# A mixer-and-experts kernel on one core: the first block's rows made by TensorE, and a token's two expert rows fetched in two turns

## What is computed

```
def _moe(h, router_w, router_b, w1, w3, w2):
    s = jax.nn.sigmoid(t @ router_w)                 # 16 experts in 4 groups
    # the best group, in it the two best experts, weights normed over the two
    gates = ...
    for e in range(N_EXPERTS):
        hid = jax.nn.silu(t @ w1[e]) * (t @ w3[e])   # 1024 -> 256
        y = y + gates[:, e:e + 1] * (hid @ w2[e])    # 256 -> 1024
```

## Time and profile before

| | us |
|---|---|
| median of 3 runs | 1379.61 |
| lowest and highest | 1375.94, 1379.90 |
| the profiled execution, its own time | 1375.57 |
| its span | 1373.8 |
| TensorE busy | 1231.2 (90%) |
| VectorE busy | 839.2 (61%) |
| ScalarE busy | 477.3 (35%) |
| GpSimd busy | 325.0 (24%) |
| mean granted TensorE clock | 0.946 of full speed |

### The profile page before, as it was taken

One profiled execution on the slowest core, in us unless ns is written; L12 is line 12 of the kernel. 1 busy time (PEld: TensorE's weight loads), 2 busy tenths in 40 slices (PEclk: granted clock), 3 DMA queues, 4 the chain that ended last, 5 costly groups with the idle time before them and its releaser, 6 DMA issues.

```text
span 1373.8 us, 24782 instructions
## 1 busy us (share of the span) xinstructions
PE 1231.2 (90%) x9304; PEld 828.1 (60%) x9304; DVE 839.2 (61%) x1616; ACT 477.3 (35%) x974; POOL 325.0 (24%) x388
## 2 busy tenths in 40 slices
PE   2989999999699999699999699999999997899980
PEld 2478867747355454484854388888888555455540
DVE  5578575484367564879325667777774425466654
ACT  4000126203165562201028544444443102466541
POOL 1000019100133333100001343444443000333433
PEclk9899899899699999899999799999999998999995
DMA  9677666482998994411110000000001405999955
GB/s 365 213 245 285 211 236 218 135 294 93 322 373 310 377 324 139 160 62 62 62 61 0 31 3 2 22 2 2 2 3 63 154 0 197 316 379 382 378 156 196
DMA packets 125163, 234.77 MB, mean 171 GB/s; under 512 B 9376, under 2 KB 77168, under 8 KB 125072
## 3 DMA queue, kind: packets, MB, share of 16 engines
q1 hardware_dynamic: 114144, 199.89, 41.9%
q0 software_dynamic: 10752, 33.56, 7.0%
q10 hardware_dynamic: 176, 0.05, 0.0%
HBM read 210.42 MB, written 23.07 MB: 170 GB/s over the span
## 4 chain that ended last, share of the span: by engine, by line
PE 74%; DVE 11%; DMA 8%; issue 3%; ACT 2%; POOL 1%; SPq 1%; DVEq 0%; POOLq 0%; ACTq 0%
PE PS L2142 14%; PE PS L2287 12%; PE PS L2108 8%; PE PS L2305 6%; PE PS L2063 5%; PE PS L2486 2%; PE PS L2468 2%; DMA xn_rows<-arena 2%; PE PS L2036 2%; PE PS L2437 2%; PE PS L2275 2%; PE PS L2374 2%; DMA arena<-in_moe_w 2%; DMA arena<-in_ada_w 2%; DVE arena L1367 2%
## 5 line engine op out<-in xcount | busy, mean ns | idle before, releaser
L2287 PE MATMUL PS<-WR,arena 128*64 128x256 f32 x1536 | 180.5, 389 | 5.2 <-ACT arena L1166 4.5
L2287 PEld LDWEIGHTS PS<-WR,arena 128*64 128x64 f32 x1536 | 108.8, 139 | 61.4 <-ACT arena L1166 6.4
L2142 PE MATMUL PS<-WR,arena 128*128 128x256 f32 x480 | 112.0, 395 | 4.2 <-DVE arena L1788 4.2
L2108 PE MATMUL PS<-WR,arena 128*128 128x512 f32 x256 | 112.6, 596 | 0.0
L2142 PEld LDWEIGHTS PS<-WR,arena 128*128 128x128 f32 x480 | 94.7, 199 | 20.1 <-DVE arena L1788 3.2
L1367 DVE SCALAR_TENSOR_TENSOR arena<-arena,cact 128x1024 f32<-128x1024 f32 x77 | 99.2, 1288 | 12.5 <-DMA arena<-in_ada_w 6.7
L1617 DVE COPY WR<-arena 128x2560 f32 x48 | 71.9, 1498 | 38.7 <-issue 29.3
L2305 PE MATMUL PS<-W,arena 128*64 128x512 f32 x384 | 92.9, 604 | 0.9 <-DVE arena L1643 0.9
L917 POOL DMA_DIRECT2D expert_rows<-arena x96 | 52.0, 541 | 156.9 <-DVE arena L1651 152.6
L2063 PE MATMUL PS<-arena,WR 128*128 128x512 f32 x192 | 86.1, 605 | 1.1 <-DVE arena L1454 1.1
L1150 ACT COPY WR<-arena 128x1536 f32 x48 | 71.0, 1480 | 42.4 <-issue 27.7
(11 more groups left out here) (370 smaller groups left out, 2262.1 us busy)
## 6 DMA issues: line engine op xcount, KB each, us to landing
arena<-in_moe_w SPq DMA_DIRECT2D x96, 1024.0 KB, 12.8
arena<-in_ada_w SPq DMA_DIRECT2D x82, 512.0 KB, 4.6
expert_rows<-arena POOLq DMA_DIRECT2D x96, 128.0 KB, 5.4
WR<-in_rwkv_w_rkv SPq DMA_DIRECT2D x6, 2048.0 KB, 7.8
WR<-in_mix_w_in SPq DMA_DIRECT2D x5, 2048.0 KB, 9.9
WR<-in_mix_w_out SPq DMA_DIRECT2D x2, 2048.0 KB, 7.9
expert_rows<-arena SPq DMA_DIRECT2D x1, 4096.0 KB, 14.3
xn_rows<-arena SPq DMA_DIRECT2D x2, 2048.0 KB, 13.8
```

Of the source, the lines that this page charges most:

```text
L2108: last = mm(out, HT[:, c, b * P:(b + 1) * P], WR[:, (first_tile + half) % 2, c, :], start=(c == 0), stop=(c == KC - 1))
L2142: last = mm(out[:, n * 256:n * 256 + 256], left, right, start=(c == 0), stop=(c == 3))
L2287: last = mm(PS[rows2[h], 2 + n, 0:2 * P].rearrange("p (m f) -> p m f", m=2), XgT[:, n, c, :], w[:, :, c, cols(h)], start=(c == 0), stop=(c ...
```

## The change

Four things are changed in the experts of both layers.

1. **The first item's rows.** As soon as `rank` is known VectorE builds `HOT0`, which marks for each token its place in item 0. TensorE then makes the rows of item 0, already turned, as 32 matmuls of 128x64 (`first_rows`, 16 for the chunks of ScalarE ahead of the list matmuls, 16 for those of VectorE behind them). The gather and the transposes of item 0 go, and so does `keep_warm(..., 5)`; `keep_warm(..., 3)` becomes `keep_warm(..., 1)`. Item 0 always belongs to expert 0, so its weights are staged without waiting for `items`.
2. **The store of `XN`** stands on SyncE's queue ahead of `landed(0)` and `load(3)`. `load(2)` now waits also for the last matmul that reads `XN` (`tx_up`). The three small loads of layer 0 move behind the experts.
3. **The order of a token's rows.** `in_order` (VectorE, 13 small instructions) puts the lower slot of a token first, with the weights to match. The lower slot is never in expert 15, so GpSimd fetches these rows (`pair_in(0)`) once the rows of experts 0 to 14 are written, and the others (`pair_in(1)`) after the last. The adds go block by block over the lower rows and then over the others.
4. **The last item's rows** are written out by SyncE and not by GpSimd.

Some semaphores of the set-up are merged, with no other change there.

```diff
+        HOT0 = tmp[:, 0, 0:NB * ROWS].rearrange("p (b r) -> p b r", b=NB)
...
             tt(A[:, 0:64], rank, m1, ALU.mult)
+            tt(sm[:, 1, 0:NB], sm[:, 0, 0:NB], b3(rank)[:, :, 0], ALU.add)
             link(tt(B[:, 0:64], rank, m2, ALU.mult))
+            tt(HOT0, io128[:, 0:ROWS].unsqueeze(1).to_broadcast([P, NB, ROWS]),
+               sm[:, 1, 0:NB].unsqueeze(2).to_broadcast([P, NB, ROWS]), ALU.is_equal).then_inc(M("idx"), 1)
...
                 load(0)
                 sp.wait_ge(*full("y", 8 * layer + 8))
                 load(1)
+                sp.wait_ge(sem("xn"), NB * (2 * layer + 2))
+                sp.dma_start(xn_dram.rearrange("(b p) f -> p b f", p=P), XN).then_inc(sem("rows_out"), 16)
                 landed(0)
                 if layer == 0:
                     sp.wait_ge(*full("mod", 5))
                 load(3)
                 landed(1)
-                sp.wait_ge(sem("xn"), NB * (2 * layer + 2))
-                sp.dma_start(xn_dram.rearrange("(b p) f -> p b f", p=P), XN).then_inc(sem("rows_out"), 16)
                 sp.wait_ge(sem("rows_out"), 16 * layer + 16)
+                sp.wait_ge(M("tx_up"), 1)
                 load(2)
                 sp.wait_ge(sem("items"), layer + 1)
...
                 landed(NEXP - 1)
+                pairs_of = sp.value_load(CN[0:1, 0:1], min_val=NEXP // 2, max_val=MAX_ITEMS // 2)
+                sp.wait_ge(sem("yt_last"), layer + 1)
+                for h in range(2):
+                    sp.dma_start(rows_of[bass.ds(pairs_of * 2 - 1, 1), h].rearrange("k r f -> (k r) f"),
+                                 Yt[rows2[h], 1, :]).then_inc(sem("last_out"), 16)
             moe(0)
+            sp.dma_start(W1L, io["rwkv_w1"][0].rearrange("(c p) f -> p c f", p=P)).then_inc(sem("lora_in"), 16)
+            sp.dma_start(A1L, io["rwkv_a1"][0].rearrange("(c p) f -> p c f", p=P)).then_inc(sem("lora_in"), 16)
+            sp.dma_start(G1L, io["rwkv_g1"][0].rearrange("(c p) f -> p c f", p=P)).then_inc(sem("lora_in"), 16)
...
-                for j in range(4):
+                for j in range(3):
                     row_out(j % 2, pairs_of * 2 + j - 4)
...
+                gp.wait_ge(sem("ranked"), layer + 1)
+                lower_out = [gp.value_load(CN[0:1, 1 + n:2 + n], min_val=NEXP // 2 - 1, max_val=MAX_ITEMS // 2)
+                             for n in range(2)]
+                def pair_in(j):
+                    for b in range(NB):
+                        gp.indirect_dma_start(CB[j][:, b, :], None, y_dram,
+                                              bass.IndirectOffsetOnAxis(ap=SLI[:, j, b:b + 1], axis=0)
+                                              ).then_inc(sem(f"pair_in{b}" if j else "lower_in"), 16)
+                for n in range(2):
+                    gp.wait_ge(M(f"row_out{n}"), lower_out[n] * 32)
+                gp.reg_add(rows_sent[0], rows_sent[0], 32)
+                gp.wait_ge(sem("rest_out"), 16)
+                pair_in(0)
+                gp.wait_ge(sem("last_out"), 32 * layer + 32)
+                for n in range(2):
+                    gp.wait_ge(M(f"row_out{n}"), rows_sent[n])
+                pair_in(1)
...
-                keep_warm(bank("lbias", layer), 3)
+                keep_warm(bank("lbias", layer), 1)
+                def first_rows(out, chunks):
+                    for k, c in enumerate(chunks):
+                        for b in range(NB):
+                            last = mm(out[:, k * ROWS:(k + 1) * ROWS], XN[:, b, c * P:(c + 1) * P], HOT0[:, b, :],
+                                      start=(b == 0), stop=(b == NB - 1))
+                    return last
+                pe.wait_ge(M("idx"), 1)
+                pe.wait_ge(sem("xn"), NB * (2 * layer + 2))
+                first_rows(PS[:, 6, :], TURN_ACT)
                 pe.wait_ge(sem("hot"), layer + 1)
                 for k in range(8):
                     last = mm(out[:, 0:MAX_ITEMS], HOTR[:, k, :], HOTI[:, k, :], start=(k == 0), stop=(k == 7))
                 last.then_inc(filled["list"], 1)
+                first_rows(PS[:, 7, :], TURN_DVE).then_inc(M("tx_up"), 1)
...
-                keep_warm(PS[:, 5, :], 5)
-                turn(0, 16)
-                pair(lambda d: d, [32, 16], first=True)
+                pair(lambda d: d, [16, 16], first=True)
...
-                for b in range(NB):
-                    v.wait_ge(sem(f"pair_in{b}"), 32 * (layer + 1))
-                    for j in range(2):
-                        if b or j:
-                            v.wait_ge(sem("x_done"), 8 * L + 2 * b + j)
-                        stt(X[:, b, :], CB[:, 2 * b + j, :], W12[:, j, b:b + 1], X[:, b, :], ALU.mult, ALU.add
-                            ).then_inc(sem("x_done"), 1)
+                v.wait_ge(sem("ranked"), layer + 1)
+                for k in range(2 * NB):
+                    j, b = k // NB, k % NB
+                    if j:
+                        v.wait_ge(sem(f"pair_in{b}"), 16 * layer + 16)
+                    elif not b:
+                        v.wait_ge(sem("lower_in"), 16 * NB * (layer + 1))
+                    if k:
+                        v.wait_ge(sem("x_done"), 8 * L + k)
+                    stt(X[:, b, :], CB[j][:, b, :], W12[:, j, b:b + 1], X[:, b, :], ALU.mult, ALU.add
+                        ).then_inc(sem("x_done"), 1)
```

More of the change, by code:

```diff
@@ L493, in route @@
             link(red(LO[0:1, 640:640 + MAX_ITEMS], it, AX, ALU.add))
+            ts(CN[0:1, 62:63], end[0:1, NEXP - 2:NEXP - 1], 1.0, None, ALU.add)
             link(ts(CN[0:1, 63:64], end[0:1, NEXP - 1:NEXP], 1.0, None, ALU.add))
@@ L886, in moe @@
                 halves = xn_dram.rearrange("s (h f) -> (s h) f", h=2)
-                gathered = gp.alloc_register(f"gathered{layer}")
+                gathered = [gp.alloc_register(f"gathered{layer}{n}") for n in range(2)]
                 indexed = [gp.alloc_register(f"indexed{layer}{n}") for n in range(2)]
@@ L918, in row_out @@
                                      ).then_inc(M(f"row_out{n}"), 16)
-                for k in range(4):
+                for k in range(1, 4):
                     gather(k % 2, k, peeled=True)
@@ L939, in moe @@
                 for n in range(2):
[L940 to L945 removed]
+                    gp.wait_ge(M(f"xg_in{n}"), gathered[n])
@@ L1167, in turned @@
+                def turned(n, turns=None):
+                    if turns is None:
+                        act.wait_ge(*full("list", layer + 1))
+                    else:
+                        act.wait_ge(M("tx_up"), turns)
+                    for k, c in enumerate(TURN_ACT):
+                        ps = PS[:, 6, k * ROWS:(k + 1) * ROWS] if turns is None else PS[:, n, k * ROWS:(k + 1) * ROWS]
+                        last = nc.scalar.activation(XgT[:, n, c, :], ps, ACT.Identity,
                                                     bias=MOD[:, L, c:c + 1], scale=MOD[:, L, 8 + c:9 + c])
@@ L1189, in moe, with expert @@
                 act.wait_ge(sem("rest_out"), 16)
-                stage_up(0, expert(0))
-                turned(0, 1)
+                stage_up(0)
+                turned(0)
+                act.wait_ge(sem("items"), layer + 1)
+                pairs_of = act.value_load(CN[0:1, 0:1], min_val=NEXP // 2, max_val=MAX_ITEMS // 2)
+                def expert(k):
+                    return act.value_load(CN[0:1, bass.ds(k + 8, 1)], min_val=layer * NEXP + 1,
+                                        max_val=layer * NEXP + NEXP)
                 stage_up(1, expert(1))
-                stage_down(0, expert(0))
+                stage_down(0)
                 pair(lambda d: d, 0, first=True)
@@ L1651, in scaled, with in_order @@
                     tt(Yt[:, n, :], PS[:, 6 + n, :], GB[:, 0:512], ALU.mult).then_inc(M("yt"), 2)
+                def in_order():
+                    first, second = SLF[:, 0:4], SLF[:, 4:8]
+                    swap, stay, parts = RF[:, 0, 0:4], RF[:, 0, 4:8], sm[:, :, 0:NB]
+                    tt(swap, first, second, ALU.is_gt)
+                    tt(RF[:, 1, 0:4], first, second, ALU.min)
+                    link(tt(RF[:, 1, 4:8], first, second, ALU.max))
+                    link(ts(stay, swap, -1.0, 1.0, ALU.mult, ALU.add))
+                    for n, (w, m) in enumerate(((0, stay), (1, swap), (0, swap), (1, stay))):
+                        last = tt(parts[:, n], W12[:, w, :], m, ALU.mult)
+                    link(last)
+                    for n in range(2):
+                        ts(CN[0:1, 1 + n:2 + n], CN[0:1, (62, 54)[n]:(62, 54)[n] + 1], 1, None, ALU.logical_shift_right)
+                    tt(W12[:, 0, :], parts[:, 0], parts[:, 1], ALU.add)
+                    tt(W12[:, 1, :], parts[:, 2], parts[:, 3], ALU.add)
+                    nc.vector.tensor_copy(SLI[:, :, :].rearrange("p j b -> p (j b)"), RF[:, 1, :]
+                                          ).then_inc(sem("ranked"), 1)
                 def pair(at, sent, k, first=False, final=False):
```

131 lines of the change are left out of this document (61 added, 70 removed).

## The result

The changed kernel took 1386.63 us (median of 5 runs, 1382.35 to 1387.76) beside 1379.61 for the kernel before: ratio 1.0045, 95% interval 1.0029 to 1.0062. A second series of 12 runs, on another occasion, gave 1.0023 (1.0011 to 1.0036). So it is slower, by 3 to 6 us. The profiled execution took 1382.35 us with a span of 1380.7, against 1375.57 and 1373.8.

The account below looks back on a forecast made before the run. Layer 1's expert stage was taken as bound by DMA and TensorE at once, layer 0's DMA as full but for a dry stretch, the end by VectorE. -5 + 8 - 2 + 0.5 = +1.5 us on 1379.6 gave 1381, range 1371 to 1388.

Parts of the forecast that it names:

- my own case: Whole kernel: first rows run at the low clock and the late load delays layer 1; 1377 to 1386 us, chance 0.5.
- my own measure of 0.3%: Whole kernel: a measurement tells about 0.3% (4.1 us) from no change.
- first rows done, layer 0 and 1: TensorE, start of expert stages: 80 records at 0.22 us take 17.5 us, ending at 364.7 and 1183.5.
- layer 0, start: Layer 0 expert stage: loads begin later, but the dry DMA stretch takes that up; -5 us, bounds -2 and -7.
- layer 0, end: End of layer 0: first add gains 1, small loads meeting the lower fetches cost 1.5; +0.5 us, bounds -1.5 and +3.
- layer 1, start: Layer 1 expert stage: `load(2)` issued 10.9 us later in a DMA-bound stage; +8 us, bounds +5.5 and +11.
- layer 1, end: End of layer 1: VectorE bounds it and the first add starts earlier, fourth fetch landing at 1347.5; gain 2, bounds 0 and 4.
- my two prices: TensorE's 128x128 weights with 64 columns: 0.107 us a record at clock 1.00, 0.226 at 0.50.
- My reason: First rows: 64-column matmuls fill about half their time, nearer to stretches that did not lift the clock; 0.22 us a record.
- The dry stretch: Layer 0, 427.5 to 433.5: DMA engines run dry as expert 9 waits for a slot; forecast to absorb the loads' lateness.
- The starvation rival: Layer 1: TensorE waits for experts, idles and drops to 1.2 GHz; +12 in place of +8, 1385 in all, chance 0.17.
- The rival that the late load is harmless: Layer 1: late load does not reach the end, the term is TensorE's +1.3; -5 in all, 1374.5, chance 0.08.

Follow-up runs that it names:

- warm_fill: Changed kernel with seven added `keep_warm` matmuls ahead of layer 1's rank product and three, not one, behind it: 1373.99 us in one run; timed again, 0.9963 to before.
- late_load: Kernel before, with expert 2's load issued only when TensorE has turned the first item's rows: ratio 1.0022 to the kernel before.
- split_load: Changed kernel, with expert 2's w2 loaded right behind expert 3's load and only w1 and w3 behind the first rows' products: ratio 0.9989 to the kernel before.
- hybrid: Changed kernel, with layer 1's first item gathered again and its `load(2)` not waiting for the first rows, layer 0 as changed: ratio 0.9971 to the kernel before.
- side_loads: Changed kernel, with layer 0's small loads and layer 1's `final_norm_g` load issued ahead of expert 2's load: ratio 1.0019 to the kernel before.

## Why the prediction came out as it did

The forecast was 1381 and no change that a measurement can tell, with an equal chance to either side; the kernel is slower by 3 to 6 us, by its first series at 1386.6. That is inside the range of 1371 to 1388, just above the 1377 to 1386 of my own case, and by my own measure of 0.3% the first series (0.45%) tells it from no change and the second (0.23%) does not. The mechanism of the clock and of the late load was right, two sizes were low, and both erred to the same side: the range held, the sum did not. By its own terms, from the two profiled executions:

| term | predicted | measured |
|---|---|---|
| first rows done, layer 0 and 1 | 364.7, 1183.5 | 364.3, 1180.7 (22.0 us behind the rank matmuls, as forecast: they began 2.5 us earlier) |
| layer 0, start | -5 | -4.4 |
| layer 0, end | +0.5 | +1.5 |
| layer 1, start | +8 | +10.4 |
| layer 1, end | -2 | -0.5 |
| sum | +1.5 | +7.3, with 0.4 from the mixer between; the spans differ by 6.9, since 0.4 comes back behind the last norm |

**The clock.** It stayed at 0.50 through all first rows in both layers. The rows took 17.3 us in layer 1, where I had 17.5, though one of my two prices was misread: of the eight records at 0.50 in the earlier trace rows only two have 64 columns, the others 48, 32 and 16. All took about as long, 0.22 to 0.23 us, and so did those of the first rows. The Trainium skill, "TensorE: Matmul & The Clock Gate", Part 1, has the rise as a matter of time under sustained matmuls. Here TensorE was busy without a gap for 17.3 us in layer 1 (1163.32 to 1180.65) and the clock did not rise, and before the change it fell under these, one column each:

```profile
334.83 7.26 PE L2036 MATMUL PS<-ones,arena 128*128 128x1 f32 x48
```

My reason was only half right: `warm_fill` shows that the same matmuls can keep a clock that is up. In the changed kernel they did not raise one that was down.

**Layer 0.** Nearly as forecast. The dry stretch has gone and the last scaled rows stand 4.4 us earlier. `load(4)` goes out 4.5 us later (377.7, against 373.2) and not the 2 that I had; the dry stretch took that up as well. In `late_load`, with the gather kept, `load(4)` goes out 5.8 us later, and the last scaled rows stand 2.2 us earlier.

**Layer 1's start, mis-sized.** I gave `load(2)` 11 us to land, took off 0.7 us for the gather saved and came to +8. It took 12.2 us (1180.7 to 1192.9), and nothing came back: the last landing is 10.0 us late for 10.6 of a late issue, 5.7 for 6.3 in `late_load`. With +10.4 it came near my upper bound of +11. `up` of item 0 took 6.64 us and not 3.67 at the low clock, but while its successor still waited for weights.

**The starvation rival** showed in its mechanism, not in its price. ScalarE waited for weights for 21.6 us in layer 1, where it had waited for 4.1, and after the longest wait TensorE idled and its clock fell once:

```profile
1292.41 1.47 ACT L1173 COPY WR<-arena 128x1536 f32 x1 [6.63 <-SPq L747]
...
1295.49 0.30 PE L2365 MATMUL PS<-ident,arena 128*128 128x128 f32 x1 [2.85 <-DVE arena L1669]
...
1297.20:1300.60 3.40, 3.40 (x20) 2.37 (x18) 2.54 (x3) 1.29 (x2) 2.79 (x3) 0.50 1.04 390
```

It cost next to nothing: the last landing is no later than the late load explains (10.0 us for 10.6), and from there to the last scaled rows pass 22.5 us, 22.2 before. That its price of 1385 lies nearer to the measured time than my 1381 speaks for the sizes, not for this rival. The rival that the late load is harmless is dead: `warm_fill` and `split_load` each win by an earlier load, and `hybrid` wins by a load as early as before.

**The ends, mis-sized.** VectorE's run from first add to last norm is 15.6 us, 16 as forecast, and all depends on the first add. I let the fourth fetch land 5.4 us after its issue, the figure of a second fetch; it took 7.8 and 6.7 (layer 0 and 1). The trace of before had a nearer one: its fourth fetch, out at 1346.50, took 6.0. And in layer 1 I placed the fetches as if `last_out` moved nothing else: SyncE now issues `final_norm_g` behind it, at 1346.59 among the fetches, where it was done before them. That this collision costs the difference is not shown: `side_loads` moved that load away and the first add of layer 1 came 0.4 us sooner, no more. In layer 0, where the same edit brought 1.9 us, the three small loads do account for it.

## What to carry to other kernels

Before a wait on TensorE's work is put ahead of a transfer, look at the granted clock where that work will run: here 64 matmul records took 14.2 us at 1.2 GHz and 7.4 at 2.4, and the transfer behind them set the end of a stage bound by its transfers. In the profiled executions the clock fell where a gap of 1.35 us stood ahead of such work, and held in three of four where two more matmuls of nothing stood in its place. At the end of a stage, move a step only together with what shares its queue: fetches issued 5 us earlier brought little until the rows that had stood behind them were issued by another engine, as soon as they were made.

## What was not expected of the hardware

- Matmuls of 64 columns, with TensorE never idle, kept a granted 1.00 for 9 us (`warm_fill`, 1163.33 to 1172.37) and did not raise 0.50 in 17 us (the changed kernel). In one of four executions without a gap the clock fell all the same.
- The gather of item 0 took 7.10 us beside a load of 3 MB and 3.55 with that load held back, and `up` started 4 us earlier (`late_load`, layer 0: 366.88 against 370.88).
- A load issued 5.4 us earlier landed 0.6 us later, with another put ahead of it and the DMA engines full (`hybrid`, layer 1).
- The mixer between the layers, the same instructions in every kernel, took 598.9 to 604.6 us. Two profiled executions can differ by more than the effect that is looked for.
